# Prompt attention of a decoder step: outputs divided by a spread and turned reciprocal, keys' turn and scans placed later, page numbers read eight at a time

## The reference

```
s = einsum('bqhd,bkhd->bhqk', q_blk, k) * scale          # scale = 64 ** -0.5
s = s + (F_blk[..., :, None] - Fh[..., None, :])         # Fh: running sum of log-forget
s = where(kpos <= qpos, s, -1e30)
p = softmax(s, axis=-1)
out = einsum('bhqk,bkhd->bqhd', p, v)
```

```
k_past = cache_k[page_table]; v_past = cache_v[page_table]     # 8 rows x 32 pages
s = einsum(q, concat(k_past, k_new)) * scale + (Fh_last - Fh)
out = einsum(softmax(s), concat(v_past, v_new))
```

## Time and profile before

| what | value |
|---|---|
| device time, median of 3 runs | 1364.9 us (1363.17 to 1365.43) |
| profiled execution, its time | 1365.37 us |
| profiled execution, its span | 1363.6 us, mean granted clock 0.991 |
| PE busy | 1313.4 us, 96% of the span, 7595 instructions |
| DVE busy | 737.1 us, 54% |
| ACT busy | 355.8 us, 26% |
| POOL busy | 608.3 us, 45% |
| DMA | 255 MB, 187 GB/s on average |

### The profile page before, as it was taken

The page is one execution under the profiler, slowest core; times in us unless marked ns, Lnnn a source line. Parts: engine busy times, 40 slices in busy tenths (PEclk is TensorE's granted clock), DMA queues, the critical chain, the costliest instruction groups (busy, mean ns, idle before and its releaser), DMA issues. The chain is left out here.

```text
span 1363.6 us, 21210 instructions
## 1 busy us (share of the span) xinstructions
PE 1313.4 (96%) x7595; PEld 1046.9 (77%) x7595; DVE 737.1 (54%) x1077; ACT 355.8 (26%) x525; POOL 608.3 (45%) x287
## 2 busy tenths in 40 slices
PE   8898999999899999999999999999999999999997
PEld 6888888888789986777777777677777776666675
DVE  4757888866666664625557374545534234311327
ACT  3524444443421342111211112021211202111116
POOL 1017686844400238475565766575662112121114
PEclk9999999999999999999999999999999999999998
DMA  7335453511135238777776877778685634477533
GB/s 245 96 120 169 133 189 109 170 59 39 60 119 197 81 118 257 259 241 243 238 253 212 281 252 240 234 238 271 198 283 165 206 127 172 175 270 277 222 138 124
DMA packets 111769, 255.02 MB, mean 187 GB/s; under 512 B 12848, under 2 KB 22961, under 8 KB 106280
## 3 DMA queue, kind: packets, MB, share of 16 engines
q1 hardware_dynamic: 102384, 247.00, 54.5%
q10 hardware_dynamic: 8320, 4.19, 1.1%
q0 software_dynamic: 960, 2.47, 0.5%
HBM read 243.73 MB, written 10.12 MB: 186 GB/s over the span
## 5 line engine op out<-in xcount | busy, mean ns | idle before, releaser
L887 POOL TENSOR_TENSOR WL<-WR,WH 128x1024 fp32r<-128x1024 f32 x55 | 132.9, 2418 | 345.4 <-ACT WH L1120 345.4
L795 POOL TENSOR_TENSOR AR<-AR,QB 128x1024 f32<-128x1024 f32 x96 | 231.9, 2429 | 98.5 <-DMA AR<-cache_k 82.6
L1547 PE MATMUL PSM<-XH,WH 128*128 128x512 f32 x672 | 214.2, 400 | 0.0
L1547 PE MATMUL PSM<-XL,WH 128*128 128x512 f32 x672 | 208.4, 391 | 0.0
L1547 PE MATMUL PSM<-XH,WL 128*128 128x512 f32 x672 | 207.5, 390 | 0.0
L2130 DVE TENSOR_TENSOR ACC<-ACC,PSM 128x512 f32<-128x512 f32 x160 | 108.4, 683 | 141.3 <-PE PSM L1557 141.1
L1547 PEld LDWEIGHTS PSM<-XH,WH 128*128 128x128 f32 x672 | 122.1, 188 | 51.2 <-issue 28.3
L1120 ACT CAST WH<-WR 128x1024 fp32r<-128x1024 f32 x55 | 57.5, 1048 | 364.5 <-PE PSM L1547 186.2
L1557 PE MATMUL PSM<-R 128*128 128x512 f32 x528 | 148.5, 390 | 0.1
L1547 PEld LDWEIGHTS PSM<-XL,WH 128*128 128x128 f32 x672 | 126.4, 188 | 27.7
L1547 PEld LDWEIGHTS PSM<-XH,WL 128*128 128x128 f32 x672 | 126.3, 188 | 27.5
(11 more groups left out here) (275 smaller groups left out, 2174.9 us busy)
## 6 DMA issues: line engine op xcount, KB each, us to landing
AR<-cache_v SPq DMA_DIRECT2D x256, 256.0 KB, 3.4
AR<-cache_k SPq DMA_DIRECT2D x192, 256.0 KB, 3.5
AR<-ws SPq DMA_DIRECT2D x37, 1024.0 KB, 6.4
WR<-ffn SPq DMA_DIRECT2D x66, 512.0 KB, 5.0
WR<-w_in SPq DMA_DIRECT2D x20, 512.0 KB, 4.4
ACC<-cache_k SPq DMA_DIRECT2D x32, 256.0 KB, 2.9
WR<-cache_k SPq DMA_DIRECT2D x32, 256.0 KB, 3.2
WR<-w_o SPq DMA_DIRECT2D x5, 1024.0 KB, 5.1
```

The source lines that it names most:

```text
L795: pool.tensor_tensor(keys, keys, QB[:].rearrange("p (o n) -> p o n", o=1).to_broadcast([P, KP, AW]), ALU.mult).then_inc(k_mul, 1)
L887: pool.tensor_tensor(lo, WR[:, raw_weight(e), :], hi.bitcast(F32), ALU.subtract).then_inc(ffn_lo, 1)
L1547: ins = pe.matmul(out[:, hc], (hi, lo)[a][:, k * P:(k + 1) * P], x[b][:, k, hc], start=(k == 0 and n == 0), stop=(k == KC - 1 and n == 2))
```

## The change

Five things are changed.

1. The scores L are turned as exp leaves them; `l_done` is gone, the turn waits on `e_done`. For each slot DVE writes the reciprocal of the row sum, spread over 64 columns, to half of a tile RB. With the weighted values PE turns RB (128x128) into columns 256 to 384 of OB. ACT copies this out of PSUM into the place of the output rows (two copies of 64x128, counted in `rows_inv`), and DVE multiplies these rows by the outputs in OB, where it copied before.
2. The turn of the next pair's keys goes from the first part of slot 11 to its end, and ACT's copy of it from slot 11 to the head of slot 12.
3. The scans go from slots 0 and 1 to 1 and 2, and "c" from slot 2 to slot 3, behind the first chunk of products and directly ahead of the first weighted values. In list O it now follows the first sampled queries.
4. Value pages are fetched by `value_pages` at unit o of `VALUES`: eight numbers are read, then eight DMAs issued, with the same waits on `v_used` ahead of the first and the fifth.
5. wfH and wfL become one tensor WF, with which RB shares its place.

```diff
-            torder += [("kn", p + 1)] if s == 11 and p + 1 < PAIRS else []
             torder += [("t", x - 1)] if 1 <= x <= SLOTS else []
+            torder += [("kn", p + 1)] if s == 11 and p + 1 < PAIRS else []
...
-        O = numbered(["ft", "c", ("q", 0), ("pv", 0), ("q", 1)] + ...
+        O = numbered(["ft", ("q", 0), "c", ("pv", 0), ("q", 1)] + ...
...
+            def value_pages(n):
+                numbers = [sp.value_load(page[0:1, bass.ds(n * CH + j, 1)], min_val=0, max_val=POOL_PAGES - 1)
+                           for j in range(2 * CH)]
+                for j, p in enumerate(numbers):
+                    if j % CH == 0:
+                        sp.wait_ge(v_used, n + j // CH - 1)
+                    sp.dma_start(VR[j // CH][:, j % CH * AW:(j % CH + 1) * AW],
+                                 t["cache_v"][bass.ds(p, 1), :, :].rearrange("a p n -> (a p) n")).then_inc(v_ld[j // CH], 16)
...
-                for c in range(2, NCH + 2):
-                    n = b * NCH + c
-                    if o == VLOAD[c - 2] and n < NB * NCH:
-                        pages(n, VR, n % 2, t["cache_v"], v_ld, v_used, n - 1)
+                if o in VALUES and u != (NB - 1) * WIN + VALUES[-1]:
+                    value_pages(b * NCH + 2 * VALUES.index(o) + 2)
...
+                if s == 12 and p + 1 < PAIRS:
+                    key_rows(p + 1)
...
+                v = x - 3
+                if v >= 0 and v % 2 == 0:
...
+                    act.wait_ge(ob_full, O["pv", v // 2] + 1)
...
+                    for a in range(2):
+                        act.copy(pair_rows(q)[hh * HD:(hh + 1) * HD, (i + a) * P:(i + a + 1) * P],
+                                 OB[a * HD:(a + 1) * HD, 2 * P:3 * P]).then_inc(rows_inv, 1)
...
-                ins.then_inc(ob_full, 1)
+                pe.wait_ge(inv_done, v + 2)
+                pe.transpose(ob[:, 2 * P:3 * P], RB[:].rearrange("p a n -> p (a n)"), ident[:]).then_inc(ob_full, 1)
...
-                    pe.wait_ge(l_done, v + 1)
+                    pe.wait_ge(e_done, v + 1)
...
-                if x < SLOTS:
-                    dve.wait_ge(e_done, x + 1)
-                    dve.reciprocal(rinv[:, x % 2:x % 2 + 1], rsum[:, x % 2:x % 2 + 1]).then_inc(inv_done, 1)
-                    dve.wait_ge(inv_done, x + 1)
-                    w = (x % RT + 1) * P
-                    dve.tensor_scalar(L[x % 2][:, 0:w], L[x % 2][:, 0:w], rinv[:, x % 2:x % 2 + 1], None, ALU.mult
-                                      ).then_inc(l_done, 1)
+                    dve.wait_ge(e_done, v + 1)
+                    if v >= 2 and v % 2 == 0:
+                        dve.wait_ge(ob_full, O["pv", (v - 2) // 2] + 1)
+                    dve.reciprocal(RB[:, v % 2, :], rsum[:, v % 2:v % 2 + 1].to_broadcast([P, HD])).then_inc(inv_done, 1)
...
+                    dve.wait_ge(rows_inv, v + 2)
                     for a in range(2):
-                        ins = dve.tensor_copy(pair_rows(q)[hh * HD:(hh + 1) * HD, (i + a) * P:(i + a + 1) * P],
-                                              OB[a * HD:(a + 1) * HD, 0:P])
+                        rows = pair_rows(q)[hh * HD:(hh + 1) * HD, (i + a) * P:(i + a + 1) * P]
+                        ins = dve.tensor_tensor(rows, rows, OB[a * HD:(a + 1) * HD, 0:P], ALU.mult)
                     ins.then_inc(ob_free, 1)
-                if x < 2:
+                if x in (1, 2):
```

More of the change, by code:

```diff
@@ L136 @@
 VALUES = (9, 21, 32, 43)
-VLOAD = tuple(o + n for o in VALUES for n in (1, 2))
 SUBTRACT0, EXPONENT0, SUM0 = 6, 8, 9
@@ L247, in build @@
         psum_row = sb("psum_row", [P, H])
-        wfH = sb("wfH", [P, KC, H], F32R)
-        wfL = sb("wfL", [P, KC, H], F32R)
+        with nc.sbuf_tensor("RB", [P, 2, HD], F32) as RB:
+            pass
+        WF = sb("WF", [P, 2, KC, H], F32R)
+        wfH, wfL = WF[:, 0], WF[:, 1]
         bfc = sb("bfc", [H, 1])
@@ L256, in build @@
         rsum = sb("rsum", [P, 2])
-        rinv = sb("rinv", [P, 2])
         mxp = sb("mxp", [P, H])
@@ L423, in build @@
         T = numbered(torder + [("sn", 0), ("sn", 1), "un"] + [("x1", i) for i in range(RT)])
-        O = numbered(["ft", "c", ("q", 0), ("pv", 0), ("q", 1)] + [("pv", n) for n in range(1, SLOTS // 2)] + ["sp", "sw"])
+        O = numbered(["ft", ("q", 0), "c", ("pv", 0), ("q", 1)] + [("pv", n) for n in range(1, SLOTS // 2)] + ["sp", "sw"])
         def pair_rows(p):
@@ L1021, in _ @@
             act.copy(XH[:, :, ROWS:XW], xs_raw.rearrange("p (k n) -> p k n", k=KC)).then_inc(small_hi, 1)
-            act.copy(wfH[:].rearrange("p k n -> p (k n)"), wf_raw).then_inc(small_hi, 1)
+            act.copy(wfH.rearrange("p k n -> p (k n)"), wf_raw).then_inc(small_hi, 1)
             entry_hi(0)
@@ L1075, in _ @@
                     act.copy(PT[1][:, 0:w], TB[:, 0:w]).then_inc(tb_free, 1)
+                v = x - 3
+                if v >= 0 and v % 2 == 0:
+                    q, r = divmod(v, STEPS)
+                    hh, i = r // RT, r % RT
+                    act.wait_ge(ob_full, O["pv", v // 2] + 1)
+                    if r == 0:
+                        if q == 1:
+                            act.wait_ge(g_st, 16 * NB)
+                        elif q == 2:
+                            act.wait_ge(pair_kept, 1)
+                        elif q == 3:
+                            act.wait_ge(k_red, EARLY)
+                    for a in range(2):
+                        act.copy(pair_rows(q)[hh * HD:(hh + 1) * HD, (i + a) * P:(i + a + 1) * P],
+                                 OB[a * HD:(a + 1) * HD, 2 * P:3 * P]).then_inc(rows_inv, 1)
                 if x < SLOTS:
@@ L1402, in _ @@
                     sample_queries((x - 3) // 2)
[L1403 to L1408, removed]
                 if x in (4, 5):
@@ L1416, in _ @@
                     turn(lambda i: VST[:, i * P:(i + 1) * P]).then_inc(tb_full, 1)
[L1417 to L1420, removed]
                 if x < SLOTS:
@@ L1423, in _ @@
                         product_step(n, m, k)
+                if x == 3:
+                    pe.wait_ge(suf_scan, 2)
+                    ob = claim_ob(O["c"])
+                    for m in range(2):
+                        ins = pe.matmul(ob[:, m * H:(m + 1) * H], cum, suftot[:, m, :], start=True, stop=True)
+                    ins.then_inc(ob_full, 1)
                 if x >= 3 and x % 2:
@@ L1435, in _ @@
                         product_step(n, m, k)
+                if s == 11 and p + 1 < PAIRS:
+                    claim_tb(T["kn", p + 1])
+                    pe.wait_ge(pt_free, 9 * p + 15)
+                    turn(lambda i: KX[(p + 1) % 2][:, i * P:(i + 1) * P]).then_inc(tb_full, 1)
                 if x >= SLOTS:
```

27 lines of the change are left out of this document (9 added, 18 removed).

## The result

The changed kernel takes 1356.79 us (median of nine runs, 1350.3 to 1359.3), the kernel before on the same chips 1363.7 (1359.43 to 1367.69). The ratio is 0.9932, interval 0.9909 to 0.9954: 9.3 us faster (6 to 12). The forecast was 1352.2, from parts that sum to -12.9.

The account below looks back on a forecast made before the run. TensorE bounds the kernel, working 1313.4 of 1363.6 us, so gains come only from its 50 us of idling or slow running. Terms -9.6, -0.3, -0.3, -3.4 and +0.7 sum to -12.9, giving 1352.2 us; range 1347 to 1360.

Parts of the forecast that it names:

- Part 1: Middle of attention: waits on DVE's scale and the row minimum go, -10.6 us; 32 added turns of reciprocals cost PE +3.4.
- Part 2: Middle of attention: with the keys' turn moved later in its slot, PE's waits behind ACT's copy go, -2.4 us.
- Part 5: Decode: eight value loads in a row remove waits for value pages, -3.4 us; later key loads cost +0.7.
- reciprocals below 0.35 us: Sign of a right forecast: DVE's 128x64 reciprocals in attention stay below 0.35 us, also beside a POOL multiply.
- no wait over 1 us at the keys' turn: Sign of a right forecast: in attention PE has no wait over 1 us at the keys' turn.
- no wait for value pages: Sign of a right forecast: PE no longer waits for value pages, where waits of 1.8 and 1.6 us stood.
- rival (a): DVE's reciprocals in attention stretch beside POOL multiplies as the scale did: +5 us, 1357; chance 0.13.
- Part 3: Start: first turn's wait falls by 2.8 us to 2.3, a new stall of 2.5 comes at the first weighted values; -0.3.
- the middle case: Start: PE's clock left as it was, neither 2.05 us less nor 2.05 us more for clock falls.
- rival (c): Both stalls at the start lower the clock (+2.05 us) and lone turns cost 0.25 each (+4.6): 1359; chance 0.09.
- Part 4: End of attention: shorter wait ahead of the output projection, -0.9 us, against later ACT copies, +0.6; net -0.3.
- rival (b): Decode: late key loads delay POOL, DVE and PE, some 17 us of late reductions; 1368.5 if all reach PE; chance 0.08.

Follow-up runs that it names:

- after_again: The changed kernel run once more, nothing altered; ratio 0.9944 to the kernel before.
- keyturn_only: Kernel before with the division by turned reciprocals and the keys' turn moved to the slot's end; scans and page loads as before; ratio 0.9894.
- scaling_only: Kernel before with the division by turned reciprocals alone; keys' turn, scans and page loads as before; 1346.72 us, ratio 0.9871.
- start_only: Kernel before with the division by turned reciprocals and the later scans and suffix product; keys' turn and page loads as before; ratio 0.9881.
- split_pages: Changed kernel with eight page numbers still read at unit o, but DMAs issued four at o+1 and four at o+2, behind the keys; ratio 0.9994.
- one_block: Changed kernel with one of its 31 blocks of eight value loads, that of unit 43, loaded as before; ratio 0.9902.
- combined: Kernel before with division, keys' turn moved, DVE's early sum of step 11 later, and later scans; page loads as before; 1345.91 us, ratio 0.9869.
- combined_v5: As combined, and in unit 23 the second value chunk is issued ahead of the keys; 1348.35 us, ratio 0.9883.
- old_pages: Changed kernel with value pages loaded as before, two chunks of four at o+1 and o+2; median 1354.69 us, ratio 0.9931.
- pages_only: Kernel before with the eight value loads in a row alone; ratio 1.0062.

## Why the prediction was right, and where not

The time fell into the range and on the right side, 4.6 us above the forecast. That it came so near is partly luck, since large errors cancel: in the paired traces the division alone gave 15.6 us in the middle where Part 1 had 7.2 (10.6 - 3.4), the keys' turn took 4.1 where Part 2 gave 2.4, and decode took 5.9 where Part 5 gave 2.7. Of the signs named for a right forecast three did not come: reciprocals below 0.35 us, no wait over 1 us at the keys' turn (1.4 in the first trace, 2.0 in the second), no wait for value pages. Of those for a wrong one, a wait of PE on the feed-forward sums came once. By its steps:

**Part 1, the scaling: right in kind, and too small.** The waits on the scale went, and those on the minimum but for a single one of 0.6 to 0.9 us in four later traces (0.7 in after_again). In the trace of before nearly all of PE's 9.0 us stood behind stretched scales: three times 1.99 us behind one of 2.81 us and 768 columns, of which the shortest takes 0.62, and twice 1.43 us behind one of 1.76 and 1024 columns, of which the shortest takes 0.75. In the paired traces the middle's idle time fell from 16.0 to 4.0 us (sum of PE's gaps), yet the middle shortened by 12.3 although the new turns were added. Those cost more than the 0.108 us taken from a run of turns: a lone turn of RB holds PE for 118.27 - 118.10 = 0.17 us, which is the step to the next turn. The 28 in the paired stretch take 4.6 us, so 32 take 5.3 instead of 3.4.

```profile
118.10 0.33 PE L1380 MATMUL PSM<-ident_sb,RB 128*128 128x128 f32 x1
...
118.27 0.49 PE L1310 MATMUL PSM<-ident_sb,AR 128*128 128x128 f32 x3
```

-12.0 and +4.6 make -7.4; the other 4.9 us are in instructions that now run closer together (products of 128x328 lost 1.4 us, those of 128x352 0.7, turns 1.7, for the same count). That instructions right behind a wait run slower is the nearest reading, and was not tested; I had counted idle time alone. With the division alone the middle gave 15.6.

The reciprocals were mis-sized, inside their bounds: 0.2 to 0.3 us forecast, 0.54 measured. DVE's line L1905, with the shortest, median and longest of 64 in ns:

```profile
L1905 DVE RECIPROCAL RB<-rsum x64: 541/544/553, 64.2 to 357.8; 128x64 f32<-128x64 f32 x64
```

They cost PE nothing, as said. From 541 to 553 ns there is no room for a wait on POOL, so rival (a) falls: at its width of 768 alone the scale had ranged from 621 to 2811. By the Trainium skill, "Vector Engine (DVE) Microarchitecture Reference", section 5.1, a reciprocal is not among the operations with a two-port mode; the trace agrees. The same section of the Trainium skill has a sentence on an element read again and again; by the trace it does not reach this operation.

**Part 2, the keys' turn: wrong.** -2.4 was forecast; the move cost 4.1 us (keyturn_only against scaling_only). Two things failed. The wait of before was no property of the place: the division alone took it away. That ACT had been late behind late minima is the nearest reading, and was not tested. And I named only ACT's copy as what stands behind the turn, not DVE's copy of the turn ahead of it, which must empty the same buffer first. In the changed kernel's timeline (start, us, engine, line, [idle before <-releaser]) it reads so:

```profile
119.84 1.22 DVE L1772 TENSOR_REDUCE PR<-WR 128x16 f32<-128x1024 f32 x1 [2.47 <-POOL WR L803]
...
120.97 0.55 DVE L1901 COPY AR<-PSM 128x384 f32<-128x384 f32 x1
...
121.58 1.09 PE L1310 MATMUL PSM<-ident_sb,ACC 128*128 128x128 f32 x8 [1.39 <-DVE AR L1901]
```

The sum waits 2.47 us for POOL's multiply, the copy L1901 stands behind it, and PE's turn of eight tiles waits 1.39 us for the copy. Before, the keys' turn stood ahead of both product chunks of its slot, and the copy that it needed was that of an earlier slot's turn. I followed ACT's queue for the waiting turn, and not DVE's.

**Part 3, the start: right in its waits, and by luck in its clock.** 2.3 us left at the first turn and 2.5 new at the first weighted values were measured at 2.34 and 2.52. The clock went in this execution as the middle case had it, one fall. By stretch: length, busy us (instructions), granted clock, DMA share, GB/s:

```profile
63.66:66.00 2.34, 2.34 (x15) 1.00 0.73 234
66.00:74.00 8.00, 8.00 (x62) 1.00 0.28 72
...
76.55:84.00 7.45, 7.45 (x36) 0.59 0.04 13
```

After the first wait the clock stayed at 1.00, where before it was 0.50; after the second it was 0.59 over 7.5 us, mostly the 1.2 GHz level. This is not so in every execution. After_again, start_only and split_pages too have the one fall; in one_block, combined, combined_v5 and old_pages the same first wait of 2.3 us was followed by a fall as well, as rival (c) had it. One_block, right behind that wait:

```profile
63.74:66.08 2.34, 2.34 (x9) 0.50 0.87 250
```

The start's length goes with the clock. Keyturn_only and scaling_only have the old start, start_only and combined the new one, in this order:

```profile
57.00:101.00 44.00, 38.83 (x287) 0.96 0.42 131
57.00:101.00 44.00, 38.83 (x259) 0.88 0.40 124
57.00:101.00 44.00, 38.73 (x287) 0.96 0.42 136
57.00:101.00 44.00, 38.73 (x257) 0.88 0.37 114
```

At 0.96 the start changed by -0.5 with the old one and by -0.5 to -0.6 with the new, at 0.88 by +1.8 and by +2.1 to +2.2. So at the same clock the new start differs from the old by 0.4 us at most, and the rest of the spread is the clock's doing. The other part of rival (c), 0.25 us for a lone turn, did not come: 0.17.

**Part 4, the end of attention: right in size, not in its way.** The wait at the output projection became 2.8 us instead of shorter; that the waits ahead of it shrank is the likely reason, not a tested one. The stretch changed by -1.7 and +0.9 in the two traces of the changed kernel, and here too the clock sets them apart. The paired stretch in the kernel before, in the changed kernel, in its second trace and in start_only:

```profile
362.00:420.00 58.00, 52.45 (x412) 0.97 0.50 180
347.67:403.99 56.32, 51.13 (x414) 1.00 0.51 183
349.93:408.81 58.88, 53.70 (x414) 0.94 0.49 175
344.24:401.82 57.58, 52.39 (x414) 0.97 0.49 180
```

The seven traces with the division that have the 0.97 of before changed by -0.1 to -0.4, about the -0.3 of the forecast; the three at 0.94 changed by +0.8 to +1.1.

**Part 5, the page numbers: wrong, and on the other side.** In pages_only what was to go went (3.4 us by the paired traces). In the changed kernel it did not all go: beside its 2.0 us, the second trace has waits for value pages of 4.0, the line below and 0.4 on L1628. The two longest (0.95 and 1.03 us in the first trace, 1.60 and 1.55 in the second) stand where the longest of before stood and at a place that had none, near 698 us of before. The second trace:

```profile
PE PSM L1630 <- DMA AR<-cache_v: 3.6, 4, 1.6
```

And the price was not 0.7. It is the mechanism of rival (b), at one place. The chain in the changed kernel's timelines, SP, POOL, DVE and PE in turn:

```profile
545.66 0.34 SPq L623 DMA_DIRECT2D WR<-ffn  x1
550.90 3.95 SPq L679 DMA_DIRECT2D AR<-cache_v  x8
556.17 0.85 SPq L506 DMA_DIRECT2D AR<-cache_k  x2
```

```profile
561.30 4.64 POOL L803 TENSOR_TENSOR AR<-AR,QB 128x1024 f32<-128x1024 f32 x2 [10.96 <-DMA AR<-cache_k]
```

```profile
563.68 1.22 DVE L1772 TENSOR_REDUCE AR<-AR 128x16 f32<-128x1024 f32 x1 [6.29 <-POOL AR L803]
564.81 1.28 DVE L2145 TENSOR_TENSOR ACC<-ACC,PSM 128x512 f32<-128x512 f32 x2
```

```profile
565.59 1.19 PE L1571 MATMUL PSM<-XH,WH 128*128 128x512 f32 x2 [4.85 <-issue]
```

SP issues a weight tile at 545.66, reads eight numbers, issues eight value loads and only then, at 556.17, the keys. POOL has waited 10.96 us for them, DVE 6.29 for POOL's product, and the adds behind that sum (L2145) are what empties PE's bank: PE stands for 4.85 us. Then it runs at half clock:

```profile
565.60:571.00 5.40, 5.40 (x13) 0.52 0.44 146
```

In the trace of before the same keys left 2.5 us after the weight tile:

```profile
556.10 0.34 SPq L623 DMA_DIRECT2D WR<-ffn  x1
558.58 0.86 SPq L506 DMA_DIRECT2D AR<-cache_k  x2
```

The step that failed is the delay of one block. I took 8.6 us for each by itself: here it is 10.5 - 2.5 = 8.0. But the weight tile ahead of it was late too. Against PE's progress (the changed kernel is 16.87 us ahead there) it left 545.66 - (556.10 - 16.87) = 6.4 us late, since its buffer is freed by POOL's low part (L895), for which SP waited 4.5 us, and that stood behind a multiply that had waited 6.49 us for keys held back by the block before:

```profile
540.88 2.39 POOL L803 TENSOR_TENSOR AR<-AR,QB 128x1024 f32<-128x1024 f32 x1 [6.49 <-DMA AR<-cache_k]
543.23 2.40 POOL L895 TENSOR_TENSOR WL<-WR,WH 128x1024 fp32r<-128x1024 f32 x1
```

So the keys left 556.17 - (558.58 - 16.87) = 14.5 us late. Delays that pass through POOL come back to SP and add up; I had compared each with the idle time next to it in the trace of before, as if the others had not happened. This place (unit 44) is not among those that rival (b) names. At the one that I worked out (near 862) the spare time was enough, as said: DVE waited 3.73 us there and PE did not.

```profile
868.11 1.22 DVE L1772 TENSOR_REDUCE SC<-AR 128x16 f32<-128x1024 f32 x1 [3.73 <-POOL AR L803]
```

What is open: by traces the new order costs some 3 to 6 us in decode against about 1 for the old one (-0.9 to +1.3, and once +4.9), and alone it makes the kernel 0.6% slower. But the times of old_pages are not better than the changed kernel's, and the old order has its own wait, the longest for value pages, of 1.8 and 2.1 us in the two traces of before and of 1.8 to 3.3 where the attention part is shorter. How often each falls in a run, one trace per kernel can't tell.

## What to carry to other kernels

When one engine's waits go, first see which of the other waits hung on the same cause before paying for their removal: the division alone took the keys' wait along, and moving the keys' turn then only cost. For a step that is moved, follow the buffer that it fills back to every reader that must empty it, and what stands ahead of that reader in its own queue. Delays on an in-order DMA queue should be summed along the loop (queue, multiply, buffer, queue), not weighed one by one against idle time of the trace before. And two traces of one stretch should be set side by side at the same granted clock: here a fall that came in one execution and not in the other moved a stretch by more than the change did.

## What the runs showed of the hardware

A 128x64 reciprocal on DVE took 0.54 us, a 128x1 one 0.158: by this, an estimate, (544 - 158) / 63 = 6.1 ns for each further element, where a pass over 512 elements took 687 ns, 1.3 ns each. The Trainium skill, "VectorE: DVE Perf Modes", section "First, the fixed hardware budget", says that the reciprocal runs as an iterative divide with a repeat count of 8; the trace agrees in kind, with between four and five times the time per element of that pass. And a wait of PE does not decide by its length alone whether the clock falls. The same wait of 2.3 us at the first turn left it at 1.00 in four traces, and in three it was 0.50 right behind it; 2.8 us at the output projection left it at 1.00 in the changed kernel's first trace, where 2.52 us at the first weighted values had brought it down.
